# Final norm of a flow-matching layer: the residual add goes from VectorE to GpSimd

## The reference

```python
h  = x * (1 + scale1) + shift1
z  = h @ w_in + b_in                      # q, k, v, o, Fourier channels, gates
x  = layer_norm(ALPHA * x + gate1 * (merged @ w_out), ln1_g, ln1_b)
h2 = x * (1 + scale2) + shift2
y2 = grouped_top2_moe(h2, ...)            # 16 experts in 4 groups, 2 per token
x  = layer_norm(ALPHA * x + gate2 * y2, ln2_g, ln2_b)

def layer_norm(x, g, b):
    mu = mean(x); var = mean(square(x - mu))
    return (x - mu) * rsqrt(var + 1e-6) * g + b
```

## Time and profile before

| | us |
|---|---|
| three runs | 1208.51, 1204.89, 1204.47 |
| median | 1204.89 |
| profiled execution, own time | 1206.22 |
| its span on the core | 1204.5 |
| busy: PE / DVE / ACT / POOL | 1131.2 / 677.0 / 475.3 / 133.6 |

### The profile page before, as it was taken

How to read it: one execution, slowest core, us unless ns; L and a number is a source line. 1 busy time by engine, 2 the same in 40 slices (tenths; PEclk the granted TensorE clock), 3 DMA queues, 4 the chain that set the end, 5 groups by cost and what they waited for, 6 DMA issues and landing times.

```text
span 1204.5 us, 15558 instructions
## 1 busy us (share of the span) xinstructions
PE 1131.2 (94%) x5915; PEld 928.3 (77%) x5916; DVE 677.0 (56%) x956; ACT 475.3 (39%) x591; POOL 133.6 (11%) x125
## 2 busy tenths in 40 slices
PE   6899999999999998999899989988999999999874
PEld 1498889999999995666766668886888888788751
DVE  0499992221222116466736239673378888888628
ACT  0531222233243323312512000214478888888614
POOL 3000000000000000000002119410010221211130
PEclk9999999999999998999999999879999999999988
DMA  8644631221112540204312141414769999999743
GB/s 338 254 175 148 229 140 49 93 71 71 70 71 70 156 140 1 70 1 112 141 70 70 70 183 79 171 40 175 279 254 391 399 403 398 404 407 397 297 160 131
DMA packets 42147, 216.12 MB, mean 179 GB/s; under 512 B 3421, under 2 KB 17993, under 8 KB 30961
## 3 DMA queue, kind: packets, MB, share of 16 engines
q1 hardware_dynamic: 34917, 190.65, 41.7%
q0 software_dynamic: 4592, 15.40, 3.7%
q10 hardware_dynamic: 2592, 9.44, 1.9%
HBM read 193.92 MB, written 21.55 MB: 179 GB/s over the span
## 4 chain that ended last, share of the span: by engine, by line
PE 72%; DVE 13%; DMA 8%; ACT 4%; issue 3%; ACTq 0%; SPq 0%; POOL 0%; POOLq 0%; DVEq 0%
PE bank L952 16%; PE bank L953 16%; PE bank L954 16%; DMA z<-w_gate_rows 6%; PE bank L1233 5%; PE bank L943 3%; PE bank L972 2%; PE bank L1102 2%; DVE z L1429 2%; DVE g_hl L1729 1%; PE bank L1120 1%; PE bank L1235 1%; ACT g_hl L838 1%; PE bank L1251 1%; PE bank L1122 1%
## 5 line engine op out<-in xcount | busy, mean ns | idle before, releaser
L952 PE MATMUL bank<-hT_hi,w_hl 128*128 128x320 f32 x832 | 258.6, 311 | 1.1 <-DVE w_hl L1385 1.1
L953 PE MATMUL bank<-hT_lo,w_hl 128*128 128x320 f32 x832 | 256.5, 308 | 0.0
L954 PE MATMUL bank<-hT_hi,w_hl 128*128 128x320 f32 x832 | 255.8, 307 | 0.0
L952 PEld LDWEIGHTS bank<-hT_hi,w_hl 128*128 128x128 f32 x832 | 156.4, 188 | 7.4 <-issue 5.2
L954 PEld LDWEIGHTS bank<-hT_hi,w_hl 128*128 128x128 f32 x832 | 156.4, 188 | 0.0
L953 PEld LDWEIGHTS bank<-hT_lo,w_hl 128*128 128x128 f32 x832 | 156.3, 188 | 0.0
L1385 DVE TENSOR_TENSOR w_hl<-r,w_hl 128x1024 fp32r<-128x1024 f32 x52 | 63.5, 1222 | 138.6 <-ACT w_hl L673 138.5
L673 ACT ACTIVATE w_hl<-r 128x1024 fp32r<-128x1024 f32 x52 | 54.8, 1055 | 80.3 <-PE bank L954 80.3
L1729 DVE TENSOR_TENSOR g_hl<-z,g_hl 128x2048 fp32r<-128x2048 f32 x32 | 72.0, 2288 | 23.2 <-ACT g_hl L838 23.2
L1729 DVE TENSOR_TENSOR d_hl<-z,d_hl 128x2048 fp32r<-128x2048 f32 x32 | 71.9, 2289 | 23.1 <-ACT d_hl L838 23.1
L708 ACT ACTIVATE z<-bank,cols 128x320 f32<-128x320 f32 (+1 forms) x52 | 27.5, 529 | 121.9 <-PE bank L954 121.8
(11 more groups left out here) (334 smaller groups left out, 2028.6 us busy)
## 6 DMA issues: line engine op xcount, KB each, us to landing
z<-w_gate_rows SPq DMA_DIRECT2D x16, 2048.0 KB, 11.4
z<-w_up_rows SPq DMA_DIRECT2D x16, 2048.0 KB, 11.1
z<-w_down_rows SPq DMA_DIRECT2D x16, 2048.0 KB, 10.9
r<-w_in_blocks SPq DMA_DIRECT2D x26, 1024.0 KB, 4.8
z<-w_ada_blocks SPq DMA_DIRECT2D x8, 2048.0 KB, 7.7
y_d<-r ACTq DMA_DIRECT2D x18, 512.0 KB, 11.3
r<-w_ada_blocks SPq DMA_DIRECT2D x3, 2048.0 KB, 14.7
y_d<-zeros SPq DMA_DIRECT2D x1, 4608.0 KB, 19.3
```

The source lines that it names most:

```text
L952: MM(dst, sta(0), mov(0), start=start, stop=False)
L953: MM(dst, sta(0), mov(1), start=False, stop=False)
L954: return MM(dst, sta(1), mov(0), start=False, stop=stop)
```

## The change

GpSimd gets five additions behind its ten gathers, each waiting for the gate pass of its tile; VectorE loses the same five additions and the wait before each. What is computed, and into which memory, stays the same. ScalarE still waits for `fin_in`, which GpSimd now counts up. Because three lines come in above, lines of VectorE's program have numbers higher by three up to the removed ones and higher by one behind them.

```diff
             for tt in range(NT):
                 for k in range(2):
                     nc.gpsimd.indirect_dma_start(yg[tt][k], None, y_d[0:SLOT_TILES * P, :], ...).then_inc(yg_loaded[tt], 16)
+            for tt in range(NT):
+                pool.wait_ge(fin_scaled, tt + 1)
+                nc.gpsimd.tensor_tensor(yg[tt][0], yg[tt][0], xr[:, tt, :], ALU.add).then_inc(fin_in, 1)
...
                     last = V.tensor_tensor(y[:, half], bank[2 * (tt % 2) + n][:, :], rows2[:, G2L + c, half], ALU.mult)
                 last.then_inc(fin_scaled, 1)
-                dve.wait_ge(fin_scaled, tt + 1)
-                V.tensor_tensor(y, y, xr[:, tt, :], ALU.add).then_inc(fin_in, 1)
```

## The result

The changed kernel's median is 1211.32 us over six runs (1208.64 to 1213.58), that of the kernel before 1204.56 over six. The ratio is 1.0055, with a 95% interval of 1.0033 to 1.0077: slower, by 4 to 9 us. The forecast was 1209.3 in a range of 1205.5 to 1213. The profiled execution took 1210.00 us with a span of 1208.3, against 1206.22 and 1204.5: +3.8 us, forecast +4.4.

A forecast was written before the change was run, and what follows sets the result against it. VectorE was taken to limit the final norm's stretch, not the whole kernel. Head +1.23, middle +1.96 and tail +1.25 sum to +4.4 us: profiled 1206.22 becomes 1210.6, median 1.3 below, forecast 1209.3, range 1205.5 to 1213.

The forecast's parts named there:

- Head: Start of the final norm: tile 0's longer GpSimd add delays ScalarE and tile 2's gate pass, +1.23 us.
- Middle: Tile 2's to tile 4's gate pass: mean passes wait for GpSimd's adds, 6.15 us a tile against 5.17, +1.96 us.
- The mechanism: Final norm's middle: VectorE passes reading two SBUF inputs wait for GpSimd's add, as L1721 did; passes reading PSUM do not.
- rival C: Final norm: scalar_tensor_tensor runs beside GpSimd without being held, +1.4 us, 1206.3; chance 0.15.
- The condition for one SBUF input: Final norm's passes: VectorE instructions with at most one SBUF input do not contend with GpSimd; no size given.
- Tail: From tile 4's gate pass to the end, a serial chain: GpSimd's longer add makes 8.15 us 9.40, +1.25 us.
- Which starts first: Middle of the final norm: GpSimd's add starts at 1185.53, VectorE's mean pass at about 1185.55, 0.02 us apart.
- Rival B: Tile 4: VectorE's mean pass gets in first, the add waits 1.3 us, +5.7 us in all, 1210.6; chance 0.25.
- Rival D: Two-tile loop: the shorter VectorE loop pays if adds last under 1.92 us; -2.0 us, 1202.9; chance 0.05.
- The total: Whole kernel: the final norm's start, middle and end sum to +4.4 us, profiled execution going from 1206.22 to 1210.6.
- above 0.5%: Whole kernel's time: slower by more than about 0.5% (6.0 us), what a measurement can tell from no change; chance 0.26.
- The cover of 1.7 us: GpSimd's queue before the first add: last gather issued by 1173.18, first gate pass ends 1174.85, so queueing costs nothing.

The follow-up runs named there:

- the run with tile 0 alone: Changed kernel with only tile 0's addition on GpSimd, the other tiles' on VectorE; first gate pass to last scale pass 29.04 us.
- the one with tile 1 alone: Changed kernel with only tile 1's addition on GpSimd, the other tiles' on VectorE; first gate pass to last scale pass 27.90 us.
- the run with the rows in PSUM: Changed kernel with ln2_g and ln2_b copied to PSUM by ScalarE, mean and scale passes reading them there in halves; final-norm stretch 30.11 us, ratio 1.0018.
- the run with tile 4 alone: Changed kernel with only tile 4's addition on GpSimd, the other tiles' on VectorE; first gate pass to last scale pass 29.03 us.
- the memset: Changed kernel with a 128x128 GpSimd memset before each add, so that VectorE's mean pass starts first; first gate pass to last scale pass 33.19 us.
- the changed one with two tiles of look-ahead: Changed kernel with tile t+2's gate pass ahead of tile t's last two passes, norm rows still in SBUF; final-norm stretch 30.38 us.
- the kernel before with both edits: Kernel before, adds on VectorE, with the norm's rows in PSUM and two tiles of look-ahead; first gate pass to last scale pass 29.04 us.

## Why the prediction was right, step by step

*Head, +1.23 forecast, +1.16 measured.* The size of the add was read from a row of 2.40; here it took 2.35. That VectorE's freed pass is worth nothing in this place is shown by the run with tile 0 alone (+1.17, the freed time goes into a longer wait for TensorE) and by the one with tile 1 alone (+0.03).

*Middle, +1.96 forecast, +1.69 measured.* The mechanism was the disputed step, carried over from L1721 and L1722 to a form of instruction that no row showed beside GpSimd. It held: 3.40 us, against 3.27 and 3.29 there, and with that rival C, no hold, is out. The prediction took the number of SBUF inputs as what separates L1721 from L1717, but the two rows differ in width as well (1024 and 512). That the second SBUF input decides is shown by the run with the rows in PSUM together with L1739 at 785.14, which is narrow and held. Forecast 6.15 us a tile, measured 6.02; the add of 2.34 makes half of the difference, the rest is that a held pass ends 1.09 us after the add where I took 1.18, although the rows that the prediction shows had 1.09 and 1.08.

*The condition for one SBUF input.* The prediction has the Trainium skill's page "SBUF — State Buffer" (section "Who interferes with whom") say that a pass with at most one SBUF input does not contend with GpSimd. The page says so only of instructions outside VectorE's two-port performance modes. The passes of this change are not touched by that, but the trace of the kernel before has a pass with one SBUF tile as input that is slower beside GpSimd:

```profile
737.84 2.77 POOL L623 TENSOR_SCALAR r<-r 128x1024 f32<-128x1024 f32 x1
```

```profile
739.97 1.18 DVE L1700 TENSOR_SCALAR r<-r,mv,rstd 128x1024 f32<-128x1024 f32 x1
...
752.53 0.81 DVE L1700 TENSOR_SCALAR r<-r,mv,rstd 128x1024 f32<-128x1024 f32 x1
```

L1700 (its other two operands are single columns) takes 1.18 us where it starts 0.64 us before the end of L623, and 0.81 us at 752.53. No row names the mode in which it ran.

*Tail, +1.25 forecast, +1.17 measured*, and +1.16 by the run with tile 4 alone.

*Which starts first.* GpSimd was forecast at 0.02 us ahead of the mean pass and was 0.02 or 0.03 ahead with the adds of tiles 2, 3 and 4, in both profiles of the changed kernel. That the starts fell this way was in part luck: the rows from which they were worked out are rounded to 0.01 us, and the prediction gave the other order 0.25. Rival B is real (33.19 us with the memset) but was not what happened. The statement of the Trainium skill's page "SBUF — State Buffer" (section "SBUF: two separate sides"), that who starts first has the shared ports for the whole instruction, agrees with both cases, to about 0.2 us: a held mean pass ends 1.09 us after the add, though alone it takes 1.28, and tile 1's (in the run with tile 1 alone) lost only 0.04 us by an overlap of 0.23.

*Rival D* needed adds under 1.92 us and none was under 2.34.

*The total.* The profiled spans differ by 3.8 us, the stretches by 4.02, the medians by 6.8 and then by 5.0 (1209.68 against 1204.7). The forecast of +4.4 comes from the profile and fits that; the medians are 0.6 to 2.4 us above it, and it lies within both intervals. That the time first came out above 0.5% (1.0055, then 1.0048), which I had given 0.26, rests on what lies ahead of the stretch; whether that is scatter or a second, smaller loss is open.

## What to carry to other kernels

Before a pass moves from VectorE to GpSimd, look at the passes that will run beside it. Here those with two SBUF inputs took turns with GpSimd's add, and 1.23 us saved cost 2.1 us of waiting; those with PSUM and SBUF as inputs ran beside it for nothing. One SBUF input alone is not proof enough, as L1700 shows, so look for rows of the same form with and without GpSimd beside them and compare their durations. A hold costs time only where the engine has none to spare: with tile 4 alone on GpSimd the hold of tile 3's mean pass cost nothing. And an engine that is slower on its own adds the difference (1.16 us here) at the first and last tile, where nothing overlaps. In the middle, a longer look-ahead can hide it, once nothing is held.

## What the runs showed of the hardware that I had not expected

The time from the first gather's issue to the first gate pass differs by 3.4 us between profiles, and goes with TensorE's granted clock in it. The same time by engine in four profiles (us, then busy us of PE, PEld, DVE, ACT and POOL, then granted clock, DMA share and GB/s): the kernel before, the changed one, the changed one with two tiles of look-ahead, and the changed one again.

```profile
1161.06:1173.56 12.50, 8.71 (x38) 5.42 (x37) 0.00 (x0) 0.00 (x0) 9.37 (x10) 0.86 0.83 287
```

```profile
1160.12:1173.35 13.23, 9.67 (x38) 5.82 (x37) 0.00 (x0) 0.00 (x0) 9.38 (x10) 0.74 0.84 299
```

```profile
1162.29:1172.54 10.25, 7.02 (x38) 4.83 (x38) 0.00 (x0) 0.00 (x0) 7.81 (x9) 1.00 0.80 263
```

```profile
1157.56:1171.18 13.62, 9.96 (x38) 5.93 (x38) 0.00 (x0) 0.00 (x0) 9.36 (x10) 0.75 0.84 294
```

The clock is a mean over the window, as a share of 2.4 GHz. At 1.00 it takes 10.3 us (10.5 in the changed kernel with the rows in PSUM), at 0.86 it takes 12.35 to 12.50, at 0.74 or 0.75 13.2 to 13.6. The second profile of the kernel before belongs to the last group, with 13.18 at 0.74, so the same kernel is found at two levels; the two fast ones are single profiles of two kernels, and whether the kernel has a part in it is not shown. The difference arises in the combining matmuls of tile 0. The same view in the changed kernel from their start, then with two tiles of look-ahead from their start to the first gate pass:

```profile
1166.88:1170.00 3.12, 3.12 (x4) 1.51 (x5) 0.00 (x0) 0.00 (x0) 2.26 (x3) 0.50 0.96 341
```

```profile
1168.73:1172.54 3.81, 3.81 (x9) 1.81 (x10) 0.00 (x0) 0.00 (x0) 2.89 (x4) 1.00 0.96 321
```

In the changed kernel TensorE had been idle for 3.56 us, the clock is 0.50 (1.2 GHz) in these 3.1 us, and it takes 6.47 us to the first gate pass. With two tiles of look-ahead it had been idle for 3.23 us, the clock is 1.00 (2.4 GHz), and it takes 3.81 us. The length of the idle time doesn't tell the two apart: with the rows in PSUM the clock stayed at 1.00 after 3.48 us, and in the kernel before with both edits it averaged 0.74 after 3.27. What decides the clock in this place is open.

A short time here didn't make an early stretch: the two profiles at 1.00 issued their first gather at 1162.3 and 1162.9, the others between 1157.5 and 1161.1. Where it was short, the first gate pass ended before the tenth gather's issue did, and the first add stood behind it in GpSimd's queue: that is the 0.33 us of the run with the rows in PSUM. The cover of 1.7 us that the prediction gave for GpSimd's queue is thus not a fixed one.
